# Gates of four tokens behind each block of the first expert table's second half, with x kept on chip

## The reference

```python
def peer_ffn(h, w_q, sub_keys, u, v):      # per token, N_KEYS = 128, PEER_TOPK = 16
    q = (hx @ w_q).reshape(TOKEN_BLOCK, PEER_HEADS, 2, PEER_HALF)
    s = jnp.einsum('nhpd,hpkd->nhpk', q, sub_keys).astype(jnp.float32)
    top_s, top_i = lax.top_k(s, PEER_TOPK)
    cand = top_s[:, :, 0, :, None] + top_s[:, :, 1, None, :]
    best_s, best_p = lax.top_k(cand.reshape(TOKEN_BLOCK, PEER_HEADS, PEER_TOPK * PEER_TOPK), PEER_TOPK)
    i1 = jnp.take_along_axis(top_i[:, :, 0], best_p // PEER_TOPK, axis=-1)
    i2 = jnp.take_along_axis(top_i[:, :, 1], best_p % PEER_TOPK, axis=-1)
    expert = (i1 * N_KEYS + i2)
    gate = jax.nn.softmax(best_s, axis=-1)
    act = jax.nn.gelu(jnp.einsum('nd,ned->ne', hx, u[expert]), approximate=False)
    return jnp.einsum('ne,ned->nd', gate * act, v[expert])
```

## Time and profile before

| | us |
|---|---|
| median of 3 runs | 2046.76 |
| lowest and highest | 2044.24, 2049.58 |
| the profiled execution | 2049.1 |
| its span, first to last instruction | 2047.3 |
| TensorE busy | 1711.4 (84%) |
| VectorE busy | 1185.3 (58%) |
| GpSimd busy | 1161.4 (57%) |
| ScalarE busy | 880.5 (43%) |

### The profile page before, as it was taken

One profiled execution on the slowest core, in us unless ns is written; L12 is line 12 of the kernel. 1 busy time (PEld: TensorE's weight loads), 2 busy tenths in 40 slices (PEclk: granted clock), 3 DMA queues, 4 the chain that ended last, 5 costly groups with the idle time before them and its releaser, 6 DMA issues.

```text
span 2047.3 us, 28946 instructions
## 1 busy us (share of the span) xinstructions
PE 1711.4 (84%) x10051; PEld 1465.9 (72%) x10051; DVE 1185.3 (58%) x1640; ACT 880.5 (43%) x1444; POOL 1161.4 (57%) x482
## 2 busy tenths in 40 slices
PE   2874796999999975699999985998959798677878
PEld 2653356999999974588888865996748654477877
DVE  6687302999300048888888877944972472245453
ACT  2233103555555579944555433436423251132332
POOL 0568004799978830088888865854924300165666
PEclk9897977999999999999999996988976799789889
DMA  7673213455555530055555552533413202333543
GB/s 271 223 261 131 83 63 132 157 177 169 184 174 185 184 102 0 0 170 192 192 194 195 192 174 98 183 121 119 155 66 123 83 1 82 123 123 124 164 134 134
DMA packets 79490, 288.75 MB, mean 141 GB/s; under 512 B 8769, under 2 KB 9281, under 8 KB 79298
## 3 DMA queue, kind: packets, MB, share of 16 engines
q1 hardware_dynamic: 78160, 283.51, 41.4%
q10 hardware_dynamic: 1266, 4.36, 0.6%
HBM read 285.75 MB, written 2.10 MB: 141 GB/s over the span
## 4 chain that ended last, share of the span: by engine, by line
PE 68%; DVE 13%; ACT 7%; POOL 4%; issue 3%; DMA 3%; ACTq 1%; SPq 0%; DVEq 0%; POOLq 0%
PE PS L322 19%; PE PS L323 18%; PE PS L324 18%; PE PS L320 6%; POOL low L1637 4%; ACT X L968 4%; DMA ring<-in_stream 2%; DVE region L1476 2%; PE PS L412 1%; DVE region L1470 1%; ACT high L808 1%; PE PS L475 1%; PE PS L731 1%; DVE hTl L1121 1%; PE PS L704 1%
## 5 line engine op out<-in xcount | busy, mean ns | idle before, releaser
L1637 POOL TENSOR_TENSOR low<-ring,high 128x1024 fp32r<-128x1024 f32 x448 | 1119.2, 2514 | 867.9 <-ACT high L808 867.8
L808 ACT ACTIVATE high<-ring 128x1024 fp32r<-128x1024 f32 x448 | 471.0, 1057 | 484.9 <-PE PS L324 375.5
L322 PE MATMUL PS<-hTh,high 128*128 128x256 f32 (+1 forms) x1728 | 500.5, 290 | 72.4 <-POOL low L1637 36.7
L323 PE MATMUL PS<-hTl,high 128*128 128x256 f32 (+1 forms) x1728 | 498.2, 288 | 0.0
L324 PE MATMUL PS<-hTh,low 128*128 128x256 f32 (+1 forms) x1728 | 497.6, 288 | 0.0
L322 PE MATMUL PS<-high,hTh 128*128 128x512 f32 (+1 forms) x960 | 382.8, 399 | 50.7 <-POOL low L1637 30.6
L322 PEld LDWEIGHTS PS<-hTh,high 128*128 128x128 f32 (+1 forms) x1728 | 331.6, 192 | 75.5 <-DVE hTl L1121 35.5
L323 PE MATMUL PS<-low,hTh 128*128 128x512 f32 (+1 forms) x960 | 379.1, 395 | 0.0
L324 PE MATMUL PS<-high,hTl 128*128 128x512 f32 (+1 forms) x960 | 378.5, 394 | 0.0
L323 PEld LDWEIGHTS PS<-hTl,high 128*128 128x128 f32 (+1 forms) x1728 | 331.4, 192 | 0.0
L324 PEld LDWEIGHTS PS<-hTh,low 128*128 128x128 f32 (+1 forms) x1728 | 330.9, 192 | 0.0
(11 more groups left out here) (251 smaller groups left out, 1592.3 us busy)
## 6 DMA issues: line engine op xcount, KB each, us to landing
ring<-in_stream SPq DMA_DIRECT2D x536, 512.0 KB, 3.3
X<-in_x SPq DMA_DIRECT2D x1, 1024.0 KB, 4.9
region<-in_band ACTq DMA_DIRECT2D x1, 1024.0 KB
result<-X ACTq DMA_DIRECT2D x1, 1024.0 KB, 6.4
X<-result ACTq DMA_DIRECT2D x1, 1024.0 KB, 5.4
result<-X SPq DMA_DIRECT2D x1, 1024.0 KB, 4.0
region<-in_skeys ACTq DMA_DIRECT2D x1, 512.0 KB
region<-in_consts ACTq DMA_DIRECT2D x1, 352.0 KB, 2.8
```

What stands on the lines that cost most here:

```text
L322: pe.matmul(out_, sh, mh, start=start, stop=False, **kw)
L323: pe.matmul(out_, sh, ml, start=False, stop=False, **kw)
L808: act.activation(high[:, b % RING, :], ring[:, b % RING, :], ACT.Copy).then_inc(rounded[b % RING], 1)
L1637: pool.tensor_tensor(low[:, b % RING, :], ring[:, b % RING, :], high[:, b % RING, :].bitcast(F32), ALU.subtract).then_inc(left[b % RING], 1)
```

## The change

`U_EARLY` becomes 64. The stage of gates is gone; its work is put behind the blocks of the second half of u: behind block 64+g TensorE issues the gates of the four tokens of group g. The second half is written out, not a loop, on all three engines.

The rows change: VectorE makes both one-hot rows by comparing iota with the indices, which it reads broadcast out of PSUM, and a third tensor as the i2 rows times the rounded gate; ScalarE makes a fourth as the i2 rows times the gate's rest (`gate_rest`, what rounding to f32r left). TensorE takes two f32r matmuls per token in place of one in float32. The rows have their own buffer `onehot`, and the i2 rows use `gate2`'s space, so `X` stays.

Weighing changes too: group g is weighed when only the blocks up to 64+g are done. Where the activation exists it is multiplied by the gate; where it isn't there yet the gate itself is stored in `region`. A later pair of blocks finds the gates of the tokens so far in `region`: its Gelu goes back to PSUM for these tokens (to `region` for the others), and VectorE multiplies (`weigh_late`). The Exp moves from behind block 79 to behind block 47.

The diff, cut to its core ("..." marks what is left out):

```diff
-        slotT = sb("slotT", [P, 3, S])
+        onehot = sb("onehot", [P, 3, 2, NB], F32R)
+        gate_rest = sb("gate_rest", [P, S])
...
-        U_EARLY = 80
-        take = carve(U_EARLY * S)
+        U_EARLY = 64
+        GROUPS = S // 4
+        take = carve(80 * S)
...
+        second = gate2.rearrange("p (b n) -> p b n", b=2)
...
+        def blocks_done(g):
+            return U_EARLY + 2 * (g // 2)
...
-            def gates(g, r=0):
-                pe.wait_ge(sem("first_rows_ready"), g + 1 + 2 * r)
-                pe.wait_ge(sem("second_rows_ready"), g + 1 + 2 * r)
-                pe.wait_ge(sem("gate_banks_free"), g + 1 + 2 * r)
+            def gates(g):
+                pe.wait_ge(sem("rows_ready"), g + 1)
+                pe.wait_ge(sem("rest_ready"), g + 1)
+                if g >= 2:
+                    pe.wait_ge(sem("gates_used"), g - 1)
+                rows, high_, rest = (fours(onehot[:, w, g % 2, :]) for w in range(3))
                 for j in range(4):
-                    last = pe.matmul(PS[:, g % 2, j * P:(j + 1) * P], onehot[:, 0, g % 2, j, :],
-                                     onehot[:, 1, g % 2, j, :], start=True, stop=True)
+                    dst = PS[:, 4 + g % 2, j * P:(j + 1) * P]
+                    pe.matmul(dst, rows[:, j, :], high_[:, j, :], start=True, stop=False)
+                    last = pe.matmul(dst, rows[:, j, :], rest[:, j, :], start=False, stop=True)
                 last.then_inc(sem("gates_placed"), 1)
...
+            for g in range(GROUPS):
+                peer_u(U_EARLY + g)
+                gates(g)
+            pe.wait_ge(sem("u_banks_free"), 4 + NK // 2)
...
-            with act.Fori(0, U_EARLY // 8) as r:
+            with act.Fori(0, U_EARLY // 8 - 2) as r:
                 for k in range(0, 8, 2):
                     gelu_u(k, r)
-            act.dma_start(out.rearrange("(t p) d -> p t d", p=P), X[:, :, :]).then_inc(sem("x_moved"), 16)
             act.wait_ge(sem("best_less_max"), 1)
             act.activation(BE.rearrange("p t h k -> p (t h k)"), BE.rearrange("p t h k -> p (t h k)"),
                            ACT.Exp).then_inc(sem("best_exp"), 1)
...
+            def second_rest(g):
+                act.wait_ge(sem("second_ready"), g + 1)
                 for j in range(4):
...
+                    ins = act.activation(fours(onehot[:, 2, g % 2, :])[:, j, :], fours(second[:, g % 2, :])[:, j, :],
+                                         ACT.Copy, scale=gate_rest[:, 4 * g + j:4 * g + j + 1])
+                ins.then_inc(sem("rest_ready"), 1)
+
+            def gelu_late(p):
+                m = U_EARLY + 2 * p
+                b = QUARTERS * AT["u0"] + m + 1
+                act.wait_ge(multiplied[b % RING], nth_split(b))
+                n = 8 * (p + 1)
+                src = PS[:, m % 8 // 2, :].rearrange("p (w s) -> p w s", w=2)
+                if n < S:
+                    act.activation(act_v[:, m:m + 2, n:S], src[:, :, n:S], ACT.Gelu)
+                act.activation(src[:, :, 0:n], src[:, :, 0:n], ACT.Gelu).then_inc(sem("late_gelu"), 1)
+
+            second_rest(0)
+            for g in range(GROUPS):
+                round_quarter(QUARTERS * AT["u0"] + U_EARLY + g + 3)
+                if g + 1 < GROUPS:
+                    second_rest(g + 1)
+                if g % 2:
+                    gelu_late(g // 2)
...
-            act.dma_start(X[:, :, :], out.rearrange("(t p) d -> p t d", p=P)).then_inc(sem("x_moved"), 16)
...
+            gate_high = onehot[:, 2, 0, 0:S]
+            link(dve.tensor_copy(gate_high, PS[:, 7, 0:S]))
+            link(dve.tensor_tensor(gate_rest[:, :], PS[:, 7, 0:S], gate_high.bitcast(F32), ALU.subtract))
+            link(dve.tensor_copy(PS[:, 7, S:2 * S], gate_high.bitcast(F32)))
+
+            def rows(g):
+                i1, i2, gate = PS[:, 6, 0:S], PS[:, 6, S:2 * S], PS[:, 7, S:2 * S]
+                tok = slice(4 * g, 4 * g + 4)
+                keys = bc(iota[:, :], 1, 4)
+                if g >= 2:
+                    dve.wait_ge(sem("gates_placed"), g - 1)
+                dve.tensor_tensor(fours(second[:, g % 2, :]), keys, bc(i2[:, tok], 2, P),
+                                  ALU.is_equal).then_inc(sem("second_ready"), 1)
+                dve.tensor_tensor(fours(onehot[:, 0, g % 2, :]), keys, bc(i1[:, tok], 2, P), ALU.is_equal)
+                dve.wait_ge(sem("second_ready"), g + 1)
+                dve.tensor_tensor(fours(onehot[:, 1, g % 2, :]), fours(second[:, g % 2, :]), bc(gate[:, tok], 2, P),
+                                  ALU.mult).then_inc(sem("rows_ready"), 1)
+
+            def weigh(g):
+                dve.wait_ge(sem("gates_placed"), g + 1)
+                n = blocks_done(g)
+                v, placed = act_v[:, :, 4 * g:4 * g + 4], PS[:, 4 + g % 2, :].rearrange("p (n i) -> p i n", n=4)
+                dve.tensor_tensor(v[:, 0:n, :], v[:, 0:n, :], placed[:, 0:n, :], ALU.mult)
+                dve.tensor_copy(v[:, n:NK, :], placed[:, n:NK, :]).then_inc(sem("gates_used"), 1)
+
+            def weigh_late(p):
+                m, n = U_EARLY + 2 * p, 8 * (p + 1)
+                dve.wait_ge(sem("late_gelu"), p + 1)
+                dve.wait_ge(sem("gates_used"), 2 * p + 2)
+                v = act_v[:, m:m + 2, 0:n]
+                dve.tensor_tensor(v, v, PS[:, m % 8 // 2, :].rearrange("p (w s) -> p w s", w=2)[:, :, 0:n],
+                                  ALU.mult).then_inc(sem("u_banks_free"), 1)
+
+            rows(0)
+            rows(1)
+            dve.wait_ge(sem("u_banks_free"), 4 + U_EARLY // 2)
+            for g in range(GROUPS):
+                weigh(g)
+                if g % 2:
+                    weigh_late(g // 2)
+                if g + 2 < GROUPS:
+                    rows(g + 2)
             dve.wait_ge(sem("u_banks_free"), 4 + NK // 2)
```

More of the change, by code:

```diff
@@ L233, in build_program, with fours @@
         QTP = M1.rearrange("p t d -> p (t d)").rearrange("p (c s) -> p c s", c=KC)
-        onehot = X[:, :, :].rearrange("p t d -> p (t d)").rearrange("p (w g j k) -> p w g j k", w=2, g=2, j=4)
+        second = gate2.rearrange("p (b n) -> p b n", b=2)
+        act_v = region[:, :].rearrange("p (i n) -> p i n", n=S)
+        def fours(buf):
+            return buf.rearrange("p (j k) -> p j k", j=4)
+        def blocks_done(g):
+            return U_EARLY + 2 * (g // 2)
         take = carve(0)
@@ L399, in _ @@
             sp_.dma_start(out.rearrange("(t p) d -> p t d", p=P), X[:, :, :]).then_inc(sem("x_moved"), 16)
-            sp_.wait_ge(sem("x_moved"), 48)
+            sp_.wait_ge(sem("x_moved"), 16)
         SMALL_ALL, LATER_ALL = 16 * 4, 16 * 5
@@ L958, in _ @@
                            ACT.Exp).then_inc(sem("best_exp"), 1)
-            act.wait_ge(sem("slots_saved"), 3)
-            with act.Fori(U_EARLY // 8, NK // 8) as r:
+            with act.Fori(U_EARLY // 8 - 2, U_EARLY // 8) as r:
                 for k in range(0, 8, 2):
                     gelu_u(k, r)
-            def first_rows(g, r=0):
-                if not (isinstance(r, int) and g < 2):
-                    act.wait_ge(sem("gates_placed"), g + 2 * r)
+            def second_rest(g):
+                act.wait_ge(sem("second_ready"), g + 1)
@@ L988, in round_weights @@
                                ACT.Copy).then_inc(sem("weights_rounded"), 1)
-            act.wait_ge(sem("gate_banks_free"), 2 + S // 4)
+            act.wait_ge(sem("gates_used"), GROUPS)
             for m in range(3):
@@ L1360, in _ @@
             dve.wait_ge(sem("slots_turned"), 1)
[L1361 to L1384, removed]
-            dve.wait_ge(sem("u_banks_free"), 4 + NK // 2)
-            dve.wait_ge(sem("x_moved"), 16)
@@ L1389, in _ @@
-            rows(0)
-            with dve.Fori(0, S // 8 - 1) as r:
-                rows(1, r)
-                weigh(0, r)
-                rows(2, r)
-                weigh(1, r)
-            rows(S // 4 - 1)
-            weigh(S // 4 - 2)
-            weigh(S // 4 - 1)
-            dve.wait_ge(sem("gate_banks_free"), 2 + S // 4)
+            gate_high = onehot[:, 2, 0, 0:S]
+            link(dve.tensor_copy(gate_high, PS[:, 7, 0:S]))
+            link(dve.tensor_tensor(gate_rest[:, :], PS[:, 7, 0:S], gate_high.bitcast(F32), ALU.subtract))
@@ L1413, in _ @@
             wait_used(dve, f"v{U_BLOCKS - 1}")
-            dve.wait_ge(sem("x_moved"), 32)
             dve.wait_ge(sem("gate2_kept"), 2)
```

7 lines of the change are left out of this document (removed).

## The result

| | before | after |
|---|---|---|
| median of 4 runs, us | 2046.97 | 1973.97 |
| lowest and highest | 2044.24, 2049.58 | 1971.55, 1976.71 |
| profiled execution | 2049.1 | 1974.88 |
| its span | 2047.3 | 1973.1 |
| stretch from block 63's last matmul to the second product | 321.4 | 247.84 |

The ratio of the times is 0.9644, with a 95% interval of 0.9626 to 0.9662. The median fell by 73.0 us, where 70.5 were forecast. The profiled executions differ by 74.2 us. 73.6 of these lie in the stretch. The rest is 3.5 us more ahead of the stretch and 4.2 less behind the second product's start.

The account below looks back on a forecast made before the run. ScalarE's one-hot rows were taken to bound the old gate stage, TensorE the new stretch. Terms 1.0 + 0.8 + 0.5 + 243.2 + 1.5 + 3.9 = 250.9 us replace 321.4, giving a median of 1976.3 us; range 1966 to 1996.

Parts of the forecast that it names:

- case A: TensorE paces the blocks with gates at 3.80 us a group; 1973 to 1983 us, chance 0.79.
- the Exp in the middle of the product: Exp moved behind block 47 takes 1.28 + 0.42 us of ScalarE, half hidden; put at 1 us (0 to 2).
- transposes, with block 63's last matmul: Before the first new group, six transposes on TensorE cost some 0.8 us at full clock.
- wait of the first group: VectorE's three small ops and group 0's rows take 3.4 us beside block 64's 2.88: 0.5 us.
- 64 periods: Each group is one block of 2.88 us plus eight gate matmuls of 0.92: 3.80 us, 243.2 in all.
- weighing at the end, and hand-over: Last group's weighing and late product 1.5 us, then 3.9 from the last gates to the second product.
- TensorE as the bound: In the new stretch TensorE's own matmuls set the period of 3.80 us; the other engines' work fits beside them.
- case B: Another engine or the round trip paces at 4.1 to 4.7 us a group: 1995 to 2034 us, chance 0.09.
- The round trip: Weighing group g-2, then rows for group g: about 3.7 us, needed after 6.7, so some 3 us of slack.
- the hole: TensorE's 5.25 us stop at block 80 in the old kernel, routing waiting for a late Exp; expected to go.
- Rival E: VectorE's new ops and GpSimd's subtraction take turns, 5.5 us a group: 38 us slower, 2085 us; chance 0.04.
- the lock: VectorE ops with two SBUF inputs are shut out while GpSimd subtracts; one PSUM input was claimed to prevent it.

Follow-up runs that it names:

- one or two operations exposed: Changed kernel with one, or two, of VectorE's three row operations per group reading only SBUF, no PSUM operand; 1969.49 us with one, 1977.70 us with two.

## Why the prediction was right

The forecast was 1976.3 us and the median is 1973.97, within the range of case A. Step by step:

| term | predicted us | measured us |
|---|---|---|
| the Exp in the middle of the product | 1.0 | 0 |
| transposes, with block 63's last matmul | 0.8 | 0.9 |
| wait of the first group | 0.5 | 0.70 |
| 64 periods | 243.2 | 240.3 |
| weighing at the end, and hand-over | 5.4 | 5.9 |
| sum | 250.9 | 247.8 |

The stretch came out 3.1 us shorter than summed, 2.9 of it in the 64 periods.

**TensorE as the bound.** Right, and shown by three runs: fewer matmuls shorten the stretch by their own spacing, one more VectorE operation leaves the period alone, three more turn the bound over to VectorE.

**VectorE.** 3.12 to 3.3 us a group, 85% busy, was too high. The busy share is 73 to 76%, from 2.74 us a group on. The recorded durations were right, 3.09 us in sum where 3.12 was put. The step that failed is adding them (and a gap of 0.03 on top): consecutive 128x512 operations start 0.60 us apart where each is recorded with 0.68. It changed nothing in the time, since this lay beside TensorE, but it made case B look closer than it is.

**ScalarE** was put at 2.7 us, and 68.37 of 100 us in 3.755 is 2.57.

**The round trip.** Some 3 us of slack were counted; TensorE waited for rows only at the first group (0.70 us), so no wait came into the 63 others. How large the slack is was not measured by itself.

**The Exp.** Half of 1.28 + 0.42 us was thought to show on TensorE. ScalarE loads a table at 504.08 and again at 505.81, behind the Exp (1.28 us each), and the product goes on, so the quarters rounded ahead hid all of it. From the first matmul of block 0 to the last of block 63 it is 188.04 us in the changed kernel, 188.05 in the kernel before and 188.06 with the Exp put behind block 63. The gain from its early place, 4.6 us, was in the prediction as the hole that goes.

**The hand-over** is 0.5 us longer than summed. Half of it lies in the weighing: TensorE's next instruction waits for the last late product and starts 1.77 us after the set (1.5 predicted), since the late product starts 0.1 us behind the copy instead of overlapping it. The other half lies in the way from there to the second product, 4.15 us. The 3.9 were counted from the recorded end of the last gates; from the spread's own start (865.95) the same way took 4.05 in the kernel before.

**Rival E** was weighed rightly and priced wrongly. The PSUM operand keeps the lock off, as the earlier trace rows had it. But with one or two operations exposed VectorE loses 0.8 to 1.1 us a group, not the 2.40 that taking turns (3.12 + 2.40) assumed, and up to 0.97 of that is hidden. Even with two operations exposed the kernel stayed at 0.9660. No run exposed all of VectorE's operations. The loss that E feared begins only where a group takes 4.9 us, which the kernel with three more operations reached.

## What to carry to other kernels

A stage bound by ScalarE or VectorE, with TensorE half idle, can be laid group by group between the blocks of a product that TensorE bounds. Its price was here TensorE's own spacing times its matmuls, and nothing else as long as every other engine's sum stayed below the period: the same work cost 2.39 us a group as a stage and 0.875 between blocks. For small f32r matmuls with fresh weights, going from 128 to 24 columns saved nothing here (0.11 us either way), and going to bf16 halved the spacing (0.056), so try the type before looking for fewer columns. In the sum for VectorE use distances from start to start (0.60 us here), not recorded durations (0.68). An operand kept in PSUM where GpSimd works beside it was worth 0 to 6.6 us here; most of the loss without it hid in VectorE's slack.

## What the runs showed of the hardware that was not expected

- An f32r matmul with its own weight load of 128 columns takes 0.109 to 0.111 us of TensorE whether it streams 24 or 128 columns; a bf16 one of 128 columns follows the one before it by 0.056, its load being recorded with 0.10 in place of 0.19 us.
- Independent 128x512 operations of VectorE overlap by 0.08 us (recorded 0.68, start to start 0.60); linked by a semaphore they are 0.72 apart.
- The lock between VectorE and GpSimd was met about once in a period, not once per exposed operation: 1480 ns in the median with one exposed, 1777 and 679 with two.
- Eights of f32r matmuls alone, 2.39 us apart, saw the granted clock at the lower level (0.50) with TensorE busy 73.54 of 90 us, where the float32 gates of the kernel before, busy 78.65 of 130, saw 0.97. The same eights between blocks saw 1.00 from 600 to 790 us.
